# A hybrid decoder layer: the last stage goes tile by tile, and the square-root table is loaded by a dummy operation

## The chip, the cores and the metric

The kernel runs on one core of one Trainium2 chip. The metric is the device time of one execution in microseconds, given as the median of several runs. One core has a matrix engine (TensorE, "PE" in the profile, its weight loads "PEld"), VectorE ("DVE"), ScalarE ("ACT"), GpSimd ("POOL") and SyncE ("SP"), which here issues nearly all transfers. The engines run on their own and meet at semaphores. TensorE writes its products into PSUM, eight banks of 128 partitions by 512 float32 words.

## The reference, cut to what matters

The layer takes 256 prompt tokens and 8 times 8 sample tokens, 320 rows of 1024 features. After a DeltaNet branch, a chunk-MLP branch and a mixture of experts, the stage that the change touches computes this:

```python
def rmsnorm(x, g):
    y = x * rsqrt(mean(x * x, axis=-1, keepdims=True) + EPS)
    return y * g

x = x + moe_ffn(h2, ...)                       # 32 experts, top 4
h3 = rmsnorm(x, norm3_g)
x = x + sigmoid(h3 @ ple_gate_w) * (p[i] @ ple_w)   # gate 1024x1024, ple 256x1024
y = rmsnorm(x, final_norm_g)                   # written out for prompt and samples
```

## The kernel before, in words

All work is float32. The 320 tokens form three tiles (`TILES`): 0 and 1 are the prompt's two halves of 128 tokens, 2 is the 64 samples. The kernel is written by hand as one instruction stream for each engine; inside a stream the order of the code is the order of execution, and a stream stops only at its own `wait_ge` on a semaphore.

The first 600 us hold both branches and the router. Then a loop (L1005 on TensorE, L1320 on ScalarE, L1765 on VectorE) goes over 35 blocks of 64 chosen tokens, with weights that SyncE streams in. The combined result of the experts stays in PSUM banks 0 to 4 (0 and 1: tile 0; 2 and 3: tile 1; 4: the samples).

What follows the loop is the tail, L1056 to L1106 on TensorE:

- `combine(nb + 1)` (L1056) adds the last block, and six transposes (L1060) turn the per-layer embedding `p` into banks 5 and 6. ScalarE copies them to `pT` (L1334).
- VectorE copies the summed `x` out of PSUM, tile 0, tile 1, samples (L1784 to L1786). ScalarE makes for each tile the sum of squares and the root (`rms`, L1120 and L1121). VectorE takes the reciprocal and scales (`normalise`, L1373 and L1374), which gives `h2`, the rows of h3 without their gain.
- The tail has ten products, numbered n = 0 to 4 twice. Tile 0 has n = 0 and 1 (the halves of the 1024 output columns), tile 1 has 2 and 3, the samples have 4, where both halves lie above each other in one bank. The first five are `p @ ple_w` (two steps of k each); the other five are the gate logits `h3 @ ple_gate_w` (eight steps each).
- `turn_h3` (L1079) transposes h2 for all three tiles, one k after the other, 24 transposes (L1087) through three banks. ScalarE evacuates even k (L1340), VectorE odd k (L1793), both with the gain `g3`. All 24 must be done before the first gate product (L1099, L1100).
- Each finished gate product goes through a sigmoid on ScalarE (L1345), a multiplication with the ple product (L1800) and an addition to `x` (L1803; for the samples L1807 to L1809, since the second half has to be moved down by 64 partitions). After the last product of a tile the final norm follows: squares and root (L1120, L1121), reciprocal and scaling (L1812, L1813), and a store by SyncE (L505). Sigmoid and root lie in different activation tables, so ScalarE has a table load at each change.

The order is fixed: gate products 0, 1, 2, 3, 4, so tile 0, tile 1, samples last.

Of the kernel before, what the change touches and what calls it, by code (L numbers as in the profile page):

```python
# [90 lines left out]
def hybrid_layer(nc, t):  # L91
    ctx = ExitStack()
    with ctx:
# [200 lines left out]
        PLE_BANKS = (5, 6, 7, 0, 1)  # L294
        H3_BANKS = (2, 3, 4)
        GATE_BANKS = (2, 3)
# [101 lines left out]
        def _(sp):  # L398
# [103 lines left out]
            for tt, (t0, tn) in enumerate(TILES):  # L502
                sp.wait_ge(sem("y_ready"), tt + 1)
                dst = t["out_yp"][0, t0:t0 + tn, :] if tt < 2 else t["out_ys"].rearrange("b s d -> (b s) d")
                sp.dma_start(dst, x[0:tn, tt, :]).then_inc(sem("stored"), 16)  # L505
# [123 lines left out]
        def _(pe):  # L629
# [436 lines left out]
            def ple_products(n, bank, lhsT, weights, kn):  # L1066

# [3 lines left out]
                for k in range(kn):  # L1071
                    if tt < 2:
                        m = mm(ps[:, bank, :], lhsT[:, k, t0:t0 + tn], weights(k, n % 2), k == 0, k == kn - 1)
                    else:
                        for g in range(2):
                            m = mm(ps[64 * g:64 * g + 64, bank, :], lhsT[:, k, t0:t0 + tn], weights(k, g), k == 0, k == kn - 1)
                return m

            def turn_h3(ks):  # L1079

                pe.wait_ge(sem("xn_ready"), 9)
                for k in ks:
                    if k >= 3:
                        odd = (k - 3) % 2
                        pe.wait_ge(sem(("hT_ready", "hT_odd_ready")[odd]), KD + odd + (k - 3) // 2 + 1)
                    for tt, (t0, tn) in enumerate(TILES):
                        m = pe.transpose(ps[:, H3_BANKS[k % 3], t0:t0 + tn], h2[0:tn, tt, k * P:(k + 1) * P], ident[0:tn, 0:tn])  # L1087
                    m.then_inc(sem("hT_done"), 1)
# [12 lines left out]
            for half in range(2):  # L1101
                pe.wait_ge(landed[uslot[half]], 16 * (before[uslot[half]] + NE + 1))
            for n in range(5):
                if n >= 2:
                    pe.wait_ge(sem("ple_sig_ready"), n - 1)
                ple_products(n, GATE_BANKS[n % 2], h3T, lambda k, g: slots[uslot[g]][:, k, :], KD).then_inc(sem("ple_done"), 1)  # L1106

# [4 lines left out]
        def _(act):  # L1112
# [222 lines left out]
            for tt in range(3):  # L1335
                act.wait_ge(sem("x_summed"), tt + 1)
# [4 lines left out]
            for n in range(5):  # L1341
                act.wait_ge(sem("ple_done"), 5 + n + 1)
                if n >= 2:
                    act.wait_ge(sem("ple_added"), n - 1)
                ACTF([g_sb, u_sb][n % 2], ps[:, GATE_BANKS[n % 2], :], ACT.Sigmoid).then_inc(sem("ple_sig_ready"), 1)  # L1345
                if n % 2 or n == 4:

                    tt = n // 2
# [493 lines left out]
```

## Time and profile before

| | us |
|---|---|
| median of 3 runs | 1681.19 |
| lowest, highest | 1679.02, 1683.44 |
| the profiled execution, its own time | 1679.4 |
| its span in the trace | 1677.6 |
| TensorE busy in the span | 1612.6 (96%) |
| TensorE's mean granted clock | 0.987 of full |

The profiled execution took 1.8 us more than its span. The tail, from the last `combine` to the end of the span, is 1611.1 to 1677.6 us. The page names for each engine its busy time, cuts the span into 40 slices, and follows the chain of work that ended last; the timeline, the stretches with their granted clock, and the chain of a window come from the trace.

### The profile page before, as it was taken

To read this page: it belongs to the slowest core of one execution; us is meant where nothing else is said; L and a number is where in the kernel's file an instruction comes from. 1 tells how busy PE (TensorE), PEld (TensorE's weight loads), DVE (VectorE), ACT (ScalarE), POOL (GpSimd) and SP (SyncE) were. 2 spreads that over 40 slices of the span, in tenths; PEclk is the share of its full clock that TensorE was granted. 3 is DMA by queue.
4 is the path that set the end of the run, shared out by engine and by line. 5 is a ranking of instruction groups with operands and counts; after the bars stand their busy time and mean duration, and the time that the engine had idled before them with its cause. 6 is when DMAs were issued, how large, how long until landed. Compare 5 with 4: busy or idle time off the path is not lost.

```text
span 1677.6 us, 21022 instructions
## 1 busy us (share of the span) xinstructions
PE 1612.6 (96%) x8487; PEld 751.6 (45%) x8488; DVE 458.6 (27%) x966; ACT 316.9 (19%) x529; POOL 112.1 (7%) x150
## 2 busy tenths in 40 slices
PE   7999999999979999999999999999999999999997
PEld 4677776776555433333333333333333333333332
DVE  3665322224771421111111112111121111112122
ACT  2224131123400131111111111111011111111123
POOL 1322101012150030000000000000000000000000
PEclk9999999999989999999999999999999999999999
DMA  4334212125854579996999999999999979949940
GB/s 160 111 121 128 102 51 102 51 101 163 255 150 168 240 285 420 417 378 258 419 419 416 419 417 418 419 416 419 417 418 419 416 311 364 419 194 408 415 146 31
DMA packets 112366, 477.32 MB, mean 285 GB/s; under 512 B 7386, under 2 KB 18067, under 8 KB 79475
## 3 DMA queue, kind: packets, MB, share of 16 engines
q1 hardware_dynamic: 109846, 467.64, 70.4%
q0 software_dynamic: 2480, 9.11, 1.9%
q8 instruction: 29, 0.48, 0.1%
q14 instruction: 11, 0.09, 0.0%
HBM read 469.72 MB, written 6.62 MB: 284 GB/s over the span
## 4 chain that ended last, share of the span: by engine, by line
PE 72%; DMA 21%; DVE 4%; issue 1%; ACT 1%; SPq 0%; ACTq 0%; DVEq 0%
PE ps L631 69%; DMA arena<-in_moe_w 20%; PE ps L981 1%; ACT arena L1307 1%; PE ps L1053 1%; DVE arena L1525 1%; PE ps L649 0%; DMA arena<-in_state_conv 0%; DVE arena L1620 0%; DVE arena L1559 0%; DVE arena L1522 0%; PE ps L1087 0%; PE ps L703 0%; DVE arena L1563 0%; DVE arena L1589 0%
## 5 line engine op out<-in xcount | busy, mean ns | idle before, releaser
L631 PE MATMUL ps<-arena 128*64 128x512 f32 (+12 forms) x7898 | 1521.4, 476 | 37.8 <-DMA arena<-in_moe_w 17.0
L631 PEld LDWEIGHTS ps<-arena 128*64 128x64 f32 (+6 forms) x7898 | 687.0, 148 | 842.0 <-issue 663.3
L1774 DVE TENSOR_SCALAR arena<-ps 128x512 f32<-128x512 f32 x35 | 24.2, 692 | 446.2 <-PE ps L631 446.2
L1322 ACT ACTIVATE arena<-arena 128x512 f32<-128x512 f32 x35 | 22.0, 630 | 475.4 <-DVE arena L1774 475.4
L1767 DVE COPY arena<-arena 96x64 bf16 x35 | 6.7, 191 | 251.6 <-PE ps L1053 248.1
L1327 ACT ACTIVATE arena<-ps 128x512 f32<-128x512 f32 x35 | 20.9, 597 | 261.6 <-PE ps L631 261.6
L1758 DVE TENSOR_TENSOR arena<-ps,arena 128x512 f32<-128x512 f32 x36 | 24.9, 692 | 122.7 <-PE ps L981 121.6
L1307 ACT ACTIVATE arena<-ps 128x512 f32<-128x512 f32 x36 | 21.5, 597 | 134.4 <-PE ps L631 134.4
L1322 ACT ACT_TABLE_LOAD x35 | 44.9, 1283 | 0.6
L1409 DVE SCALAR_TENSOR_TENSOR arena<-arena 128x344 f32<-128x344 f32 x48 | 35.5, 740 | 1.7
L1120 ACT ACTIVATE arena<-arena 128x1024 f32<-128x1024 f32 (+1 forms) x12 | 12.6, 1052 | 113.8 <-DVE arena L1644 103.3
L1190 ACT ACTIVATE arena<-ps 128x320 f32<-128x320 f32 x32 | 14.0, 436 | 98.0 <-PE ps L631 97.8
L1769 DVE TENSOR_SCALAR arena<-arena 128x128 f32<-128x128 f32 (+1 forms) x105 | 29.8, 342 | 0.0
L981 PE MATMUL ps<-arena 128*128 128x128 f32 x144 | 23.6, 287 | 3.7
L1780 DVE TENSOR_TENSOR arena<-arena 128x512 f32<-128x512 f32 x35 | 24.3, 694 | 1.2
L1777 DVE SCALAR_TENSOR_TENSOR arena<-arena 128x512 f32<-128x512 f32 x35 | 24.3, 693 | 1.2
L1053 PEld LDWEIGHTS ps<-arena 128*128 128x128 f32 (+1 forms) x105 | 11.8, 140 | 27.8 <-issue 27.8
L1775 DVE TENSOR_SCALAR arena<-ps 128x512 f32<-128x512 f32 x35 | 23.8, 681 | 0.0
L1503 DVE TENSOR_TENSOR arena<-arena,ps 128x512 f32<-128x512 f32 (+1 forms) x11 | 7.6, 687 | 59.2 <-PE ps L631 59.2
L1031 PE MATMUL ps<-arena 128*128 128x128 f32 x140 | 23.0, 287 | 0.0
L581 POOL TENSOR_TENSOR arena<-arena 128x512 f32<-128x512 f32 (+1 forms) x15 | 18.9, 1266 | 55.7 <-PE ps L631 27.0
L1053 PE MATMUL ps<-arena 128*128 128x128 f32 (+1 forms) x105 | 22.5, 292 | 0.0
(249 smaller groups left out, 649.3 us busy)
## 6 DMA issues: line engine op xcount, KB each, us to landing
arena<-in_moe_w SPq DMA_DIRECT2D x192, 2048.0 KB, 18.3
arena<-in_w_in SPq DMA_DIRECT2D x16, 2048.0 KB, 11.1
arena<-in_state_delta POOLq DMA_DIRECT2D x16, 512.0 KB, 6.3
arena<-in_w_proj_a SPq DMA_DIRECT2D x2, 2048.0 KB, 11.1
out_sd_s<-arena SPq DMA_DIRECT2D x8, 512.0 KB, 5.8
arena<-in_w_proj_b SPq DMA_DIRECT2D x2, 2048.0 KB, 11.5
arena<-in_w_out SPq DMA_DIRECT2D x2, 2048.0 KB, 7.8
arena<-in_ple_gate_w SPq DMA_DIRECT2D x2, 2048.0 KB, 16.0
```

Of the source, the lines that this page charges most:

```text
L631: return pe.matmul(out, lhsT, rhs, start=first, stop=last, skip_group_check=True)
L981: m = pe.transpose(ps[:, TURN_B, P * j:P * j + P], xsel[:, P * j:P * j + P], ident)
L1053: m = pe.transpose(ps[:, TURN_B, t0:t0 + tn], Pg[0:tn, tt, :], ident[0:tn, 0:tn])
L1307: ACTF(xsel, ps[:, TURN_B, :], ACT.Copy).then_inc(sem("xsel_ready"), 1)
L1322: ACTF(s_sb, g_sb, ACT.Sigmoid, scale=ALPHA).then_inc(sem("glu_sig_ready"), 1)
L1409: ch.link(STT(a, z[:, i:i + CW], g_conv[:, i, n:n + 1], a, ALU.mult, ALU.add))
L1758: TT(xselT.rearrange("p (g j) s -> p g j s", g=2), ps[:, TURN_B, :].rearrange("p (j g s) -> p g j s", j=4, g=2), g2.rearrange("p (g j a) - ...
L1769: m = TS(Pg[0:tn, tt, :], cst("slot", tn), posb[0:tn, tt, bass.ds(b, 1)], gateb[0:tn, tt, bass.ds(b, 1)], ALU.is_equal, ALU.mult)
L1774: TS(g_sb, ps[:, GATE_B, :], LIMIT, None, ALU.min).then_inc(sem("glu_gate_ready"), 1)
L1775: TS(u_sb, ps[:, UP_B, :], LIMIT, -LIMIT, ALU.min, ALU.max).then_inc(sem("glu_up_ready"), 1)
L1777: STT(u_sb, u_sb, 1.0, g_sb, ALU.add, ALU.mult).then_inc(sem("glu_up_ready"), 1)
L1780: TT(a_sb, u_sb, s_sb, ALU.mult).then_inc(sem("act_ready"), 1)
```

## The change

Only the tail is touched.

- The tiles go in the order 2, 0, 1 (samples first) in the copies out of PSUM, in the norm, in the transposes, in the gate products (n = 4, 0, 1, 2, 3) and in the stores.
- h3 is transposed tile by tile, eight transposes each, into whole banks: samples into bank 4, tile 0 into 2 and 3, tile 1 into 4 and 7. VectorE alone evacuates them, with one instruction for a bank. ScalarE's four evacuations are gone.
- TensorE's stream is: ple 4, turn samples, ple 0, first half of gate 4, turn tile 0, second half of gate 4, ple 1, gate 0, turn tile 1, ple 2, ple 3, gate 1, gate 2, gate 3.
- Each product has its own bank or a bank that a finished product left, so the gate products wait on `ple_added` instead of on the sigmoids.
- ScalarE runs a root of one column (`ACTF(warm, eps_col, ACT.Sqrt)`) right after the loop and after each sigmoid that ends a tile; nothing reads its result.

```diff
+        TAIL_TILES = (2, 0, 1)
+        TAIL_ORDER = (4, 0, 1, 2, 3)
+        PLE_BANKS = {4: 7, 0: 5, 1: 6, 2: 0, 3: 1}
+        LOGIT_BANKS = {4: 4, 0: 2, 1: 3, 2: 5, 3: 6}
+        H3_BANKS = {2: (4,), 0: (2, 3), 1: (4, 7)}
...
-            for n in range(5):
-                if n == 0:
-                    pe.wait_ge(sem("pT_ready"), 2)
-                elif n == 3:
-                    pe.wait_ge(sem("x_summed"), 1)
-                elif n == 4:
-                    turn_h3(range(3))
-                ple_products(n, PLE_BANKS[n], pT, lambda k, g: wp[:, k, 512 * g:512 * g + 512], 2).then_inc(sem("ple_done"), 1)
-            turn_h3(range(3, KD))
-            pe.wait_ge(sem("hT_ready"), KD + KD // 2)
-            pe.wait_ge(sem("hT_odd_ready"), KD + 1 + KD // 2)
...
+            def turn_h3(tt):
+                tn = TILES[tt][1]
+                banks = H3_BANKS[tt]
+                per = KD // len(banks)
+                for k in range(KD):
+                    m = pe.transpose(ps[:, banks[k // per], tn * (k % per):tn * (k % per) + tn], h2[0:tn, tt, k * P:(k + 1) * P], ident[0:tn, 0:tn])
+                    if k % per == per - 1:
+                        m.then_inc(sem("hT_done"), 1)
+
+            pe.wait_ge(sem("pT_ready"), 2)
+            ple_product(4)
+            pe.wait_ge(sem("xn_ready"), 7)
+            turn_h3(2)
+            ple_product(0)
...
+            pe.wait_ge(sem("hT_odd_ready"), KD + 2)
+            gate_logits(4, range(KD // 2))
+            pe.wait_ge(sem("x_summed"), 3)
+            pe.wait_ge(sem("xn_ready"), 8)
+            turn_h3(0)
+            gate_logits(4, range(KD // 2, KD))
+            ple_product(1)
+            pe.wait_ge(sem("hT_odd_ready"), KD + 4)
+            gate_logits(0)
+            pe.wait_ge(sem("ple_added"), 1)
+            pe.wait_ge(sem("xn_ready"), 9)
+            turn_h3(1)
+            ple_product(2)
+            ple_product(3)
+            gate_logits(1)
+            pe.wait_ge(sem("hT_odd_ready"), KD + 6)
+            pe.wait_ge(sem("ple_added"), 2)
+            gate_logits(2)
+            pe.wait_ge(sem("ple_added"), 3)
+            gate_logits(3)
...
+            ACTF(warm, eps_col, ACT.Sqrt)
             act.wait_ge(sem("pT_done"), 1)
...
-            for k in range(0, KD, 2):
-                act.wait_ge(sem("hT_done"), 2 * KD + 1 + k + 1)
-                ACTF(h3T[:, k, :], ps[:, H3_BANKS[k % 3], 0:TOK], ACT.Copy, scale=g3[:, k:k + 1]).then_inc(sem("hT_ready"), 1)
...
+            for i, n in enumerate(TAIL_ORDER):
+                act.wait_ge(sem("logits_done"), 2 + i + 1)
+                if i >= 2:
+                    act.wait_ge(sem("ple_added"), i - 1)
+                ACTF([g_sb, u_sb][i % 2], ps[:, LOGIT_BANKS[n], :], ACT.Sigmoid).then_inc(sem("ple_sig_ready"), 1)
                 if n % 2 or n == 4:
+                    ACTF(warm, eps_col, ACT.Sqrt)
+                    act.wait_ge(sem("ple_added"), i + 1)
+                    rms(n // 2, h2[:, n // 2, :])
...
+            ch(dve.tensor_copy(x[0:64, 2, 0:512], ps[0:64, 4, :]))
+            dve.tensor_copy(x[0:64, 2, 512:1024], ps[64:128, 4, :]).then_inc(sem("x_summed"), 1)
             for tt in range(2):
                 dve.tensor_copy(x[:, tt, :], ps[:, 2 * tt:2 * tt + 2, :].rearrange("p a c -> p (a c)")).then_inc(sem("x_summed"), 1)
-            ch(dve.tensor_copy(x[0:64, 2, 0:512], ps[0:64, 4, :]))
-            dve.tensor_copy(x[0:64, 2, 512:1024], ps[64:128, 4, :]).then_inc(sem("x_summed"), 1)
             ch.wait()
+            dve.wait_ge(sem("x_summed"), 3)
+            def h3_turned(tt, done):
+                t0, tn = TILES[tt]
+                banks = H3_BANKS[tt]
+                per = KD // len(banks)
+                for a, bank in enumerate(banks):
+                    dve.wait_ge(sem("hT_done"), 2 * KD + 1 + done + a + 1)
+                    TT(h3T[:, per * a:per * a + per, t0:t0 + tn], ps[:, bank, :].rearrange("p (k s) -> p k s", k=per),
+                       g3[:, per * a:per * a + per].rearrange("p (k a) -> p k a", a=1).broadcast_to([P, per, tn]), ALU.mult).then_inc(sem("hT_odd_ready"), 1)
+            normalise(3, 2, h2, TAIL_TILES)
+            h3_turned(2, 0)
+            normalise(3, 0, h2, TAIL_TILES)
+            h3_turned(0, 1)
+            normalise(3, 1, h2, TAIL_TILES)
...
+                if i == 0:
+                    h3_turned(1, 3)
```

How the order moves, first on TensorE at the head of the tail. L631 is the helper that issues every product, L1060 turns `p`, L1087 turns h3. A product of the prompt's tiles has 128 rows, one of the samples is written as 64x512 twice. Before:

```order
L1060 MATMUL ps<-arena 128x64
L631 MATMUL ps<-arena 128x512 x8
L1087 MATMUL ps<-arena 128x128 x2
L1087 MATMUL ps<-arena 128x64
...
L631 MATMUL ps<-arena 64x512 x4
...
L631 MATMUL ps<-arena 128x512 x32
L631 MATMUL ps<-arena 64x512 x16
```

In the changed kernel the same engine has (L634 and L1063 are the old L631 and L1060, L1095 is the new transposes):

```order
L1063 MATMUL ps<-arena 128x64
L634 MATMUL ps<-arena 64x512 x4
L1095 MATMUL ps<-arena 128x64 x8
L634 MATMUL ps<-arena 128x512 x2
L634 MATMUL ps<-arena 64x512 x8
L1095 MATMUL ps<-arena 128x128 x8
L634 MATMUL ps<-arena 64x512 x8
L634 MATMUL ps<-arena 128x512 x10
L1095 MATMUL ps<-arena 128x128 x8
L634 MATMUL ps<-arena 128x512 x28
```

The ple product of the samples alone now stands ahead of the first transposes, and the 24 transposes are three groups of eight with products between them.

ScalarE after the last gate product, before (L1345 is the sigmoid, L1120 the squares, L1121 the root):

```order
L1345 ACTIVATE arena<-ps 128x512 [waits ple_done]
L1120 ACTIVATE arena<-arena 64x1024 [waits ple_added]
L1121 ACT_TABLE_LOAD
L1121 ACTIVATE arena<-arena 64x1 [waits act_chain]
L93 UNCONDITIONAL_BRANCH
```

and in the changed kernel (L1362, L1139 and L1140 are those three, L1365 is the dummy root):

```order
L1362 ACTIVATE arena<-ps 128x512 [waits ple_added,logits_done]
L1365 ACT_TABLE_LOAD
L1365 ACTIVATE arena<-arena 128x1
L1139 ACTIVATE arena<-arena 128x1024 [waits ple_added]
L1140 ACTIVATE arena<-arena 128x1 [waits act_chain]
L93 UNCONDITIONAL_BRANCH
```

The table load has moved ahead of the wait for `ple_added` and of the squares.

## Rows read from the trace of the kernel before

**Rows 1.** The page, costliest groups: count, busy us, mean ns, idle before.
```profile
L1758 DVE TENSOR_TENSOR arena<-ps,arena 128x512 f32<-128x512 f32 x36 | 24.9, 692 | 122.7 <-PE ps L981 121.6
```

**Rows 2.** Chain that ended last, head of the tail: start us, us, what.
```profile
1616.17 7.11 PE ps L631 x16
1623.28 1.57 PE ps L1087 x9
1624.85 1.87 PE ps L631 x8
1626.71 2.87 PE ps L1087 x15
1629.58 0.69 issue
1630.27 36.41 PE ps L631 x96
```

**Rows 3.** Stretches: PE, PEld, DVE, ACT, POOL busy, granted clock, DMA share, GB/s.
```profile
1614.00:1616.00 2.00, 1.23 (x8) 0.67 (x6) 1.87 (x2) 0.74 (x3) 0.00 (x0) 1.00 0.00 0
...
1628.00:1630.00 2.00, 1.58 (x9) 0.81 (x7) 0.94 (x2) 1.36 (x3) 0.00 (x0) 1.00 0.00 0
1630.00:1632.00 2.00, 1.73 (x2) 0.84 (x3) 0.17 (x1) 0.87 (x1) 0.00 (x0) 0.55 0.00 0
```

**Rows 4.** Timeline of ScalarE, 1638 to 1647 us: sigmoids of gate products 0 and 1.
```profile
1639.07 0.60 ACT L1345 ACTIVATE arena<-ps 128x512 f32<-128x512 f32 x1 [8.20 <-PE ps L631]
1645.94 0.60 ACT L1345 ACTIVATE arena<-ps 128x512 f32<-128x512 f32 x1 [6.27 <-PE ps L631]
```

**Rows 5.** Timeline, 1614 to 1620 us, VectorE and ScalarE: start, us, what.
```profile
1614.13 2.36 DVE L1784 COPY arena<-ps 128x1024 f32<-128x1024 f32 x2 [10.81 <-PE ps L631]
...
1615.91 1.06 ACT L1120 ACTIVATE arena<-arena 128x1024 f32<-128x1024 f32 x1
...
1616.40 0.67 DVE L1785 COPY arena<-ps 64x512 f32<-64x512 f32 x1
...
1617.08 1.28 ACT L1121 ACT_TABLE_LOAD   x1
...
1618.38 0.29 ACT L1121 ACTIVATE arena<-arena 128x1 f32<-128x1 f32 x1
...
1618.77 0.16 DVE L1373 RECIPROCAL arena<-arena 128x1 f32<-128x1 f32 x1 [0.97 <-ACT arena L1121]
...
1618.97 0.75 DVE L1374 TENSOR_SCALAR arena<-arena 128x1024 f32<-128x1024 f32 x1
```

**Rows 6.** TensorE's timeline near 141 us, and half-microsecond stretches as in Rows 3.
```profile
141.05 4.45 PE L703 MATMUL ps<-arena 128*27 128x128 f32 x24
...
144.50:145.00 0.50, 0.50 (x4) 0.40 (x3) 0.00 (x0) 0.50 (x1) 0.00 (x0) 0.50 0.60 233
145.00:145.50 0.50, 0.50 (x4) 0.45 (x3) 0.00 (x0) 0.49 (x3) 0.00 (x0) 0.60 0.74 254
```

**Rows 7.** Chain that ended last, end of the tail: start us, us, what.
```profile
1666.70 0.61 ACT arena L1345
...
1668.05 0.42 DVE arena L1807
...
1668.51 0.69 DVE arena L1808
...
1669.94 1.15 ACT arena L1120 x2
...
1671.11 1.28 ACT L1121
```

**Rows 8.** Issues of the stores: KB each, median us from issue to landing; and the last store.
```profile
out_yp<-arena SPq DMA_DIRECT2D x2, 512.0 KB, 2.6
...
out_ys<-arena SPq DMA_DIRECT2D x1, 256.0 KB, 2.9
...
1674.22 0.51 SPq L505 DMA_DIRECT2D out_ys<-arena  x1
```

More of the change, by code:

```diff
@@ L500, in _ @@
             sp.dma_start(fng, t["final_norm_g"].rearrange("(a d) -> a d", a=1).broadcast_to([P, D])).then_inc(sem("ple_in"), 16)
-            for tt, (t0, tn) in enumerate(TILES):
-                sp.wait_ge(sem("y_ready"), tt + 1)
+            for i, tt in enumerate(TAIL_TILES):
+                t0, tn = TILES[tt]
+                sp.wait_ge(sem("y_ready"), i + 1)
                 dst = t["out_yp"][0, t0:t0 + tn, :] if tt < 2 else t["out_ys"].rearrange("b s d -> (b s) d")
@@ L1064, in _, with products @@
             wp = slots[uslot[2]].rearrange("p k n -> p (k n)")[:, 0:2048].rearrange("p (k n) -> p k n", k=2)
-            def ple_products(n, bank, lhsT, weights, kn):
+            def products(n, bank, lhsT, weights, ks, last):
                 tt = min(n // 2, 2)
                 t0, tn = TILES[tt]
-                for k in range(kn):
+                for k in ks:
                     if tt < 2:
-                        m = mm(ps[:, bank, :], lhsT[:, k, t0:t0 + tn], weights(k, n % 2), k == 0, k == kn - 1)
+                        m = mm(ps[:, bank, :], lhsT[:, k, t0:t0 + tn], weights(k, n % 2), k == 0, k == last)
@@ L1074, in ple_products @@
                     else:
                         for g in range(2):
-                            m = mm(ps[64 * g:64 * g + 64, bank, :], lhsT[:, k, t0:t0 + tn], weights(k, g), k == 0, k == kn - 1)
+                            m = mm(ps[64 * g:64 * g + 64, bank, :], lhsT[:, k, t0:t0 + tn], weights(k, g), k == 0, k == last)
                 return m
[L1079 to L1088, printed above, removed]
@@ L1090, in _, with ple_product @@
-            for n in range(5):
-                if n == 0:
-                    pe.wait_ge(sem("pT_ready"), 2)
-                elif n == 3:
-                    pe.wait_ge(sem("x_summed"), 1)
-                elif n == 4:
-                    turn_h3(range(3))
-                ple_products(n, PLE_BANKS[n], pT, lambda k, g: wp[:, k, 512 * g:512 * g + 512], 2).then_inc(sem("ple_done"), 1)
-            turn_h3(range(3, KD))
-            pe.wait_ge(sem("hT_ready"), KD + KD // 2)
-            pe.wait_ge(sem("hT_odd_ready"), KD + 1 + KD // 2)
+            def ple_product(n):
+                products(n, PLE_BANKS[n], pT, lambda k, g: wp[:, k, 512 * g:512 * g + 512], range(2), 1).then_inc(sem("ple_done"), 1)
@@ new lines, in gate_logits @@
+            def gate_logits(n, ks=range(KD)):
+                m = products(n, LOGIT_BANKS[n], h3T, lambda k, g: slots[uslot[g]][:, k, :], ks, KD - 1)
+                if ks[-1] == KD - 1:
+                    m.then_inc(sem("logits_done"), 1)
+            def turn_h3(tt):
[6 more added lines that the diff above has]
+                        m.then_inc(sem("hT_done"), 1)
@@ L1368, in _, with normalise @@
             dve.memset(ab, 0.0).then_inc(sem("zeroed"), 1)
-            def normalise(k, tt, dst):
+            def normalise(k, tt, dst, order=(0, 1, 2)):
                 tn = TILES[tt][1]
-                dve.wait_ge(sem("rms_ready"), 3 * (k - 1) + tt + 1)
+                dve.wait_ge(sem("rms_ready"), 3 * (k - 1) + order.index(tt) + 1)
                 ch.link(dve.reciprocal(rstd[0:tn, tt:tt + 1], rstd[0:tn, tt:tt + 1]))
```

35 lines of the change are left out of this document (8 added, 27 removed).

## The prediction, made before the changed kernel ran

> **What bounds the kernel now.** I read the chain of work that ended last first. At its end it lies in the tail: TensorE from 1616.17 us to the last gate product at 1630.27 + 36.41 = 1666.68 [rows 2], with one hole of 0.69 us before the gate products, then eleven microseconds that alternate between ScalarE and VectorE [rows 7] and end in the store of the samples, issued at 1674.22 [rows 8], with the span's end at 1677.6. So two things count: what makes TensorE reach its last product earlier, and what lies behind that product. Whatever ScalarE and VectorE do beside the gate products costs nothing. Everything ahead of 1614 us is the same in both kernels, so of 1680 us only some 65 are open.
>
> The second view is the stretches with their granted clock. The gate products begin at half clock (1.2 of 2.4 GHz): 0.55 as the mean of 1630 to 1632 us, after 1.00 up to 1630 [rows 3]. What TensorE did before it fell was fifteen transposes and the hole [rows 2]. The price comes from the sigmoids. Gate product 1 took 1645.94 - 1639.07 = 6.87 us; product 0 took 1639.07 - 1630.27 = 8.80 [rows 4]. The last product, with its drain, takes 36.41 - 8.80 - 3 x 6.87 = 7.00, so the slow stretch cost 8.80 - 7.00 = 1.80 us.
>
> **The head of the tail on TensorE.** The ten products are the same, and so is the number of transposes, 24, which took 1.57 + 2.87 = 4.44 us [rows 2]. Four things differ.
>
> The hole before the gate products goes: -0.69. Product, turned bank and evacuation are now apart. The samples' bank is evacuated during ple 0, tile 0's two banks during gate 4's second half, tile 1's during ple 2, ple 3 and gate 1. One such evacuation is a 128x512 operation of VectorE out of PSUM with a broadcast factor, 0.69 us [rows 1], against two steps of ple 0, which take 7.11 / 4 = 1.8 us. Without that cover it would cost 0.7 for each group. Next in line is `ple_added`: the samples' additions are over about 4 us after gate 4, and TensorE asks for them after 1.8 + 6.9 us of products. VectorE then waits for the turning of tile 1 with the samples' final norm queued behind it; that norm is needed only by a store, with four gate products still to come.
>
> A new wait comes in. After ple 4, TensorE wants the samples' h2. It is free at 1616.17 + 1.87 = 1618.04. VectorE has first its three copies, 2 x 0.67 for the samples and 2.36 for tiles 0 and 1, from 1614.13: until 1617.9 with gaps. ScalarE's squares can start at 1615.91 as now and take 1.15 with the read of the sum [rows 5, 7], and the root, its table now loaded before, 0.29: ready at 1617.4. So VectorE is later. Reciprocal 0.16 and scaling 0.75 [rows 5] end at 1618.9. TensorE waits 0.9 us; queued behind it are all the gate products. If the root came with its load (1.28) [rows 5], this would be 1.7, and if the copies cost nothing, 0.4. I take 0.9, since every duration in it has a row.
>
> Cutting the work into more pieces costs some filling at each change between transposes and products. Of the four ple products in a row each took 7.11 / 4 = 1.78; ple 4, between transposes, took 1.87 [rows 2]: 0.1 at such a place. Two more such places than before make 0.2. From below: the samples' eight transposes have a quarter of the data, and if they ran in half the time of the others (4.44 x 8 / 24 / 2) it would be 0.7 less. I take +0.2, by the row that it is nearest to.
>
> The slow stretch. Before, fifteen transposes stood together just ahead of the hole. Now no group is longer than eight transposes (about 1.5 us), and each has products on both sides. The quietest place is new: the transposes of `p`, the wait for `pT` until 1616.17 [rows 2], ple 4, 0.9 of waiting, eight small transposes, then ple 0. The first half of that exists already, and the clock stayed at 1.00 from 1614 to 1616 with TensorE busy for 1.23 of 2 us [rows 3]. So I let the slow stretch go: -1.80. The bounds are -1.80 and 0 (it comes at the new quiet place).
>
> The Trainium skill has a rule here ("TensorE: Matmul & The Clock Gate", Part 4, PE-mode transpose): transposes do not count as busy for the clock in the way products do. By that rule the chip would see only ple 4 between 1614 and 1620 us, and the slow stretch would move there, not go: the sum would be 1.80 worse.
>
> The trace bears out both sides. The clock fell here after transposes and a hole [rows 2, 3]. But at 145 us it came back, from 0.50 to 0.60 and then 1.00, while TensorE had done nothing but the transposes of L703 for four microseconds [rows 6]. So transposes alone can bring the clock back, and I don't take the fall for certain.
>
> Head: -0.69 + 0.9 + 0.2 - 1.80 = -1.4, so the last product ends at 1665.3.
>
> **Behind the last product.** With the samples last there were, after the sigmoid, a multiplication, the move by 64 partitions (0.42 + 0.03 gap), two additions (0.69 each) and after the squares the table load of 1.28 [rows 7]. With tile 1 last, the move and one addition go: -0.45 - 0.71. The load goes from this place: -1.28. It is now issued behind the sigmoid, with the dummy root: 1.28 + 0.29 + 0.02 = 1.59, beside a multiplication and an addition on VectorE (0.69 + 0.70 + gaps = 1.43). The cover is short by 0.16: +0.16. The last store is 512 KB in place of 256 KB, but the large ones landed in 2.6 us and the small one in 2.9 [rows 8]: -0.3; the bounds are -0.3 and +0.3, should twice the bytes count after all. Squares and scaling are as long for 64 partitions as for 128 (1.06 us for a 128-row tile against 1.15 with the read of the sum for 64) [rows 5, 7]. Sum: -2.6.
>
> The skill ("ScalarE: Activation LUTs", What ACT_TABLE_LOAD costs) gives a switch of tables 1283 ns and a drain of about 1380 ns more. With that the dummy would stick out by 1.5 us, and this part would bring 1.2. The trace has the 1.28 but no drain: the root follows the load at 1617.08 + 1.28 + 0.02 = 1618.38 [rows 5].
>
> **The sum.** -1.4 - 2.6 = -4.0 us. Against the profiled execution's own 1679.4 that is 1675.4. That execution lies 1.8 below the median of the three runs, and nothing says that the next ones will be as low, so I put the sum against the median: 1681.19 - 4.0 = 1677.2.
>
> **The rivals.**
>
> The slow stretch stays, at the new quiet place or wherever it falls: no gain from it, -2.2 us, 1679.0. For it: between 1614 us and ple 0, nearly six microseconds, only ple 4's 1.9 are products. Against it: the stretch before 1616 us kept its clock, and the fall at 1630 us had a longer row of transposes without a product between. It would give the same time if the executions of before mostly don't have the stretch.
>
> Every group of transposes now costs one: three slow stretches in place of none, -4.0 + 3 x 1.80 = +1.4, 1682.6, slower than before. It decides with the third stretch: one leaves 2.2 of the gain, two leave 0.4, three turn it over. For it: the clock fell behind transposes. Against it: the groups at tile 0 and 1 have at least 3.4 us of products on each side.
>
> The change brings the lower bounds: small transposes in half the time, no filling, the dummy covered: -4.0 - 0.7 - 0.2 - 0.16 = -5.1, 1676.1. For it: only the smaller amount of data; against it: every group of transposes in the chain took 0.17 to 0.19 us each, small ones included.
>
> The dummy roots don't do their work (the head's root still carries its load, or the one at the end sits in the way): 0.8 more in the head and 1.3 at the end, -1.9, 1679.3. The order of the compiled code speaks against it: load and dummy stand ahead of the waits.
>
> **How the numbers follow.** Forecast, stretch gone: 0.50. Stretch stays: 0.28. Lower bounds: 0.12. Dummies without effect: 0.04. Three stretches: 0.06. Likeliest is 1677.2. The range reaches over the second case and the third and adds the median's own scatter (three runs of before lie 4.4 us apart, so a median of three moves by 1 or 2): 1674.5 to 1681.5. A measurement of this kernel can tell about 0.3% from no change, which is 5.0 us, so faster means under 1676.1. That takes half of the lower-bound case (0.06), a fifth of the forecast's (0.10) and a little of the others': 0.18. Slower by over 0.3% (over 1686.2) needs more than three stretches: 0.02. The rest, 0.80, is within 0.3%.
>
> **What would show it.** Right: TensorE stands still for about 0.9 us ahead of the samples' transposes, released by VectorE's scaling; no wait before any gate product; a granted clock of 1.00 from 1616 us to the last product, which ends some 50 us after `combine`, 1.4 sooner than before; behind it 10.9 - 2.6 = 8.3 us to the end of the span, with a load beside VectorE's multiplication. Wrong: a granted clock near 0.5 around 1620 us, a wait before a gate product, a store that takes 3 us or more, or an end behind the last product of more than 9.5 us.

## The result, and the profile after

The changed kernel took 1674.60 us (median of 6 runs, 1673.28 to 1675.03), the kernel before 1681.38 us beside it; the ratio is 0.9959, with a 95% interval of 0.9948 to 0.9971. That is 6.8 us less, where 4.0 were forecast. The measured time lies at the low edge of the range (1674.5 to 1681.5), and it is faster by more than 0.3%, a case that had a chance of 0.18.

Two later comparisons on other occasions gave 0.9981 (0.9970 to 0.9992) and 0.9963 (0.9950 to 0.9977). Over all three, 21 runs of the changed kernel have a median of 1674.6, and 66 runs of before, taken beside all experiments, 1680.0: 5.4 us.

One execution of either program scatters by several microseconds, and the traces show where: the first block of the loop turns its activations (L1031) at 612.8 us in the trace of before, at 616.3 in a second trace of the same program, at 618.2 in another kernel with the same front. The loop behind it then takes about as long in each of them (997.6 to 999.3 us to the last combine, in the ten traces with this loop and this combine). So I compare tails, from the start of the last combine to the end of the span. Before that is 1677.6 - 1611.09 = 66.5 us.

The page of the changed kernel, its first line and the costliest group:

```profile
span 1672.8 us, 21024 instructions
...
PE 1612.1 (96%) x8487; PEld 752.2 (45%) x8488; DVE 456.4 (27%) x967; ACT 315.5 (19%) x529; POOL 112.1 (7%) x150
```

The chain that ended last, changed kernel, from the last combine on (start us, us, what; the answer to [rows 2] and [rows 7]):

```profile
1612.20 3.02 PE ps L634 x12
...
1619.32 0.76 DVE arena L1391
...
1620.12 0.71 PE ps L1095 x8
1620.83 5.50 PE ps L634 x20
1626.33 1.02 PE ps L1095 x8
1627.35 12.37 PE ps L634 x36
1639.72 0.87 PE ps L1095 x8
1640.59 24.05 PE ps L634 x56
...
1664.66 0.60 ACT arena L1362
...
1665.28 1.28 ACT L1365
...
1666.57 0.20 ACT arena L1365
1666.78 1.12 ACT arena L1139 x2
...
1667.92 0.30 ACT arena L1140
...
1668.45 1.29 DVE arena L1843
```

The tail is 1672.8 - 1612.20 = 60.6 us, 5.9 less. L634 are the products and L1095 the transposes of h3. From 1620.12 on TensorE has no gap up to the last product, at 1664.64; before the first group of transposes stands VectorE's scaling (L1391), for which TensorE waited 0.90 us, in the row of TensorE's own timeline:

```profile
1620.12 0.71 PE L1095 MATMUL ps<-arena 64*128 64x64 f32 x8 [0.90 <-DVE arena L1391]
```

The granted clock of the changed kernel, at the new quiet place and where the old slow stretch was (columns as in [rows 3]):

```profile
1618.00:1620.00 2.00, 1.22 (x6) 0.17 (x2) 1.88 (x3) 1.94 (x7) 0.00 (x0) 1.00 0.00 0
1620.00:1622.00 2.00, 1.88 (x11) 1.25 (x12) 1.16 (x4) 1.95 (x4) 0.00 (x0) 1.00 0.00 0
...
1630.00:1632.00 2.00, 2.00 (x9) 0.71 (x6) 0.39 (x1) 1.00 (x2) 0.00 (x0) 1.00 0.00 0
```

It stays at full speed, where [rows 3] has 0.55.

From the start of the combine to the end of the last product there are 52.4 us in place of 55.6, so -3.15 (forecast -1.4). The terms are the holes, -0.69 + 0.90; the transposes, 0.71 + 1.02 + 0.87 = 2.60 us in place of 4.44, so -1.84; and the products, 43.9 us (the three groups of the chain and 1.94 for ple 4) in place of 45.4 [rows 2], so -1.54, the slow stretch and some filling together. Behind the last product there are 8.16 us in place of 10.92, so -2.76 (forecast -2.6).

### The profile page after: what moved, and what is told of

It reads as the page before. It is cut to its first block, busy times and chain, and to the rows that moved or that the text cites. A ratio compares the mean times of both kernels' runs of the same rounds, so it can differ in the third digit from the quotient of the medians.

```text
span 1672.8 us, 21024 instructions
## 1 busy us (share of the span) xinstructions
PE 1612.1 (96%) x8487; PEld 752.2 (45%) x8488; DVE 456.4 (27%) x967; ACT 315.5 (19%) x529; POOL 112.1 (7%) x150
## 4 chain that ended last, share of the span: by engine, by line
PE 71%; DMA 21%; DVE 4%; issue 1%; ACT 1%; POOL 1%; SPq 0%; POOLq 0%; DVEq 0%; ACTq 0%
PE ps L634 68%; DMA arena<-in_moe_w 20%; PE ps L984 1%; ACT arena L1326 1%; PE ps L1056 1%; POOL arena L626 1%; DVE arena L1542 1%; PE ps L652 0%; DMA arena<-in_state_conv 0%; DVE arena L1576 0%; DVE arena L1637 0%; DVE arena L1539 0%; PE ps L706 0%; DVE arena L1580 0%; DVE arena L1606 0%
## 5 line engine op out<-in xcount | busy, mean ns | idle before, releaser
L634 PE MATMUL ps<-arena 128*64 128x512 f32 (+12 forms) x7898 | 1522.5, 476 | 35.4 <-DMA arena<-in_moe_w 16.1
L634 PEld LDWEIGHTS ps<-arena 128*64 128x64 f32 (+6 forms) x7898 | 687.8, 148 | 839.3 <-issue 663.1
L1139 ACT ACTIVATE arena<-arena 128x1024 f32<-128x1024 f32 (+1 forms) x12 | 12.6, 1051 | 107.7 <-DVE arena L1661 101.7
## 6 DMA issues: line engine op xcount, KB each, us to landing
arena<-in_w_proj_b SPq DMA_DIRECT2D x2, 2048.0 KB, 11.5
```

Source lines behind the costliest of these rows:

```text
L634: return pe.matmul(out, lhsT, rhs, start=first, stop=last, skip_group_check=True)
```

## The experiments

Twelve runs were made, on three occasions: nine edited kernels, the changed kernel twice and the kernel before once. The table has the wall times and the tails of the traces, each from one execution; "clock" says whether TensorE's granted clock fell to half inside the tail, ahead of the last product. No tail is given where the edit moves the combine, from whose start it is counted.

| kernel | median us (runs) | ratio to before beside it, 95% | tail us | clock |
|---|---|---|---|---|
| before_again | 1683.17 (1) | | 66.4 | fell |
| e_dummies_only | 1679.57 (10) | 0.9992, 0.9982 to 1.0002 | 65.1 | fell |
| e_no_dummies | 1678.37 (10) | 0.9991, 0.9981 to 1.0000 | 62.7 | full |
| e_together | 1676.97 (8) | 0.9977, 0.9966 to 0.9988 | 61.2 | full |
| after_again | 1676.44 (10) | 0.9981, 0.9970 to 0.9992 | 60.6 | full |
| e_grouped_rows | 1681.43 (10) | 1.0002, 0.9991 to 1.0014 | 64.0 | full |
| e_patterns | 1679.19 (1) | | 60.6 | full |
| e_filled_head | 1675.76 (10) | 0.9972, 0.9960 to 0.9983 | | fell |
| after_third | 1673.79 (5) | 0.9963, 0.9950 to 0.9977 | 60.6 | full |
| e_loop_rows | 1673.63 (6) | 0.9967, 0.9955 to 0.9979 | 60.6 | full |
| e_best | 1672.78 (6) | 0.9958, 0.9944 to 0.9973 | | full |
| e_best_loop | 1670.08 (5) | 0.9945, 0.9931 to 0.9959 | | full |

**before_again**: the kernel before, not edited.

> The kernel before, unchanged, for a second trace. The result of the change was 1674.6 us against 1681.4 (-6.8) where -4.0 was forecast, while the two profiled tails (from the last combine to the end of the span) differ by 66.5 - 60.6 = 5.9. If the slow stretch of the clock after the transposes belongs to this order of work, the second trace has it again, between 15 and 24 us after the combine, and the tail is again 66 to 67 us. If it comes by chance, the tail is either 66.5 without a change of time elsewhere or about 64.7 with a granted clock of 1.00 throughout. If more than one stretch can fall into the tail (which would explain why the executions of before scatter over 4.4 us and those of after over 1.8), it is up to 68.3.

The tail is 66.4 us again, and the slow stretch again follows the transposes. The scatter is not in the tail but ahead of it: this trace is 1.7 us later than the first by 567 us and 3.5 later by 616. What differs on the way are slow stretches of the clock between 574 and 600 us, where the router's small operations leave TensorE waiting; they lie at other places in the two traces (around 582 and 590 us in the first, around 576, 586 and 594 in the second).

**e_dummies_only**: before, plus the dummy roots.

```diff
+            ACTF(warm, eps_col, ACT.Sqrt)
             act.wait_ge(sem("pT_done"), 1)
...
                     tt = n // 2
+                    ACTF(warm, eps_col, ACT.Sqrt)
                     act.wait_ge(sem("ple_added"), n + 1)
```

> The kernel before plus only the dummy roots (behind the loop and behind the last sigmoid of each tile). Theory: at the head nothing changes, since TensorE has ple products to do until h2 is there; at the end the load of 1.28 us leaves the chain, covered by the four VectorE operations of the samples (2.6 us): -1.3 us, about 1680.1, and the root follows the squares within 0.05 us. Rival one (a switch of tables costs a drain besides its load, which the trace doesn't show): -2.7. Rival two (a dummy delays the squares by itself): -1.0 or less.

The tail is 65.1 us, 1.3 to 1.4 less, as expected from the load's own 1.28. The median is 0.5 us less (1680.07 to 1679.57), inside its noise. Rival one, the drain, asked for 2.7 and is out by the tails; the medians alone could not tell. The chain has squares and root with nothing between:

```profile
1672.01 1.16 ACT arena L1120 x2
1673.17 0.02 issue
1673.19 0.30 ACT arena L1121
```

The slow stretch is in this trace too. So it is in three of three traces of this order of work.

**e_no_dummies**: the changed kernel without them (the two `ACTF(warm, ...)` lines of the diff above taken out of it).

> The changed kernel without its dummy roots. Theory: at the end the load is back in the chain, +1.28, and the dummy's own delay of about 0.06 goes: +1.2; at the head the first root comes at 1619.8 in place of 1618.5 in the trace's time, while VectorE is free at 1619.1, so TensorE waits 1.6 in place of 0.9: +0.7. Sum +1.9, about 1676.5. Rival (the head is not bound by the root): +1.2, about 1675.8, and the wait stays at 0.9.

The tail is 62.7, so +2.1 against 60.6 (expected +1.9). Both parts are in the chain: ScalarE's load now stands ahead of the samples' root and holds VectorE back, and it stands again behind the last squares.

```profile
1618.86 1.02 ACT arena L1139 x2
...
1619.90 1.28 ACT L1140
...
1621.20 0.30 ACT arena L1140
```

So the dummies are worth 2.1 us in the changed order, and 1.3 in the old one, where nothing at the head waits for the root. The median lies 1.7 below before where the tails differ by 3.7; a difference of 2 between the two ways of looking is more than I can account for. The 2.1 us rest on the traces.

**e_together**: ple products first, then all transposes tile by tile, then the gate products.

```diff
-        LOGIT_BANKS = {4: 4, 0: 2, 1: 3, 2: 5, 3: 6}
-        H3_BANKS = {2: (4,), 0: (2, 3), 1: (4, 7)}
+        LOGIT_BANKS = {4: 3, 0: 2, 1: 4, 2: 5, 3: 6}
+        H3_BANKS = {2: (4,), 0: (2, 3), 1: (4, 2)}
...
+            for n in (4, 0, 1, 2, 3):
+                if n == 2:
+                    pe.wait_ge(sem("x_summed"), 3)
+                ple_product(n)
+            pe.wait_ge(sem("xn_ready"), 9)
+            turn_h3(2)
+            turn_h3(0)
+            pe.wait_ge(sem("hT_odd_ready"), KD + 3)
+            turn_h3(1)
...
+            pe.wait_ge(sem("hT_odd_ready"), KD + 6)
+            gate_logits(4)
...
```

> The changed kernel with its five ple products first, then all 24 transposes (still tile by tile), then the five gate products; three banks are used twice. Theory, that products between the groups keep the clock up: the slow stretch is back, +1.8; a hole of 1.4 us before the gate products and up to 0.5 at the third group, while the new wait of 0.9 is gone: +1.0. Sum +2.8, about 1677.4, with a granted clock near 0.5 behind the transposes. Rival, that the shorter time of the transposes alone (2.6 us for 24, against 4.4 before) keeps the clock: +1.0, about 1675.6, and a clock of 1.00. The transposes take 2.6 us under both; if they take 4.4, it was the products between them that made them fast.

My theory fell here. From the last ple product at 1631.38 to the first gate product at 1635.54 there are 4.16 us of transposes and holes, longer than the 3.56 of before, and the clock stayed full (columns as in [rows 3]):

```profile
1630.00:1632.00 2.00, 2.00 (x13) 0.94 (x11) 0.00 (x0) 0.00 (x0) 0.00 (x0) 1.00 0.00 0
1632.00:1634.00 2.00, 1.64 (x14) 1.41 (x14) 1.89 (x3) 0.00 (x0) 0.00 (x0) 1.00 0.00 0
1634.00:1636.00 2.00, 0.96 (x8) 0.50 (x8) 1.29 (x2) 0.00 (x0) 0.00 (x0) 1.00 0.00 0
```

The tail is 61.2, +0.6 against the changed kernel; the rival had said +1.0. So "products between the transposes" brings 0.6 us, the evacuations that it covers, and is not needed for the full clock in this trace. The medians agree with the tails: 1676.97, and 1676.44 for the changed kernel in after_again.

**after_again** and **after_third**: the changed kernel, not edited.

> The changed kernel once more, beside the same runs of the kernel before as the three others. The tails of the traces differ by 5.9 us (66.5 to 60.6); the first comparison gave 6.8. If the 0.9 above the tails is scatter of the first 600 us (the first block of the loop turned its rows at 612.8 to 618.0 us in six traces of kernels whose front is the same), this run is 5.9 within about 1 below before, and its tail is 60.6 within 0.2. If the change moves something ahead of the tail, it is again 6.8 or more.

The tail is 60.6 again, as expected. The difference of the medians is 3.4 us where 5.9 within 1 was expected, with an interval of 1.3 to 5.0, which doesn't hold the 5.9 of the tails; in this set the changed kernel scattered from 1674.25 to 1680.11.

> The changed kernel beside the three others, as their base on this chip. So far its tail is 60.6 us in two traces against 66.5 and 66.4 of before, and the differences of the medians were 6.8 and 3.4 us. The front of the same program ends anywhere from 612.8 to 618.4 us in ten traces, with slow stretches of the clock in other places each time, so a median of ten runs moves by about 1. Expected: 5.9 below before, within 1.5.

The median is 5.5 us below before, and the tail 60.6. Two of the three comparisons have the 5.9 in their interval, and all runs together give 5.4.

**e_grouped_rows**: before, with the transposes of each round taken tile by tile.

```diff
...
-                    for tt, (t0, tn) in enumerate(TILES):
-                        m = pe.transpose(ps[:, H3_BANKS[k % 3], t0:t0 + tn], h2[0:tn, tt, k * P:(k + 1) * P], ident[0:tn, 0:tn])
-                    m.then_inc(sem("hT_done"), 1)
+                for tt, (t0, tn) in enumerate(TILES):
+                    for k in part:
+                        m = pe.transpose(ps[:, H3_BANKS[k % 3], t0:t0 + tn], h2[0:tn, tt, k * P:(k + 1) * P], ident[0:tn, 0:tn])
+                        if tt == 2:
+                            m.then_inc(sem("hT_done"), 1)
```

> The kernel before, with its transposes in the same three rounds of k, the same banks and the same evacuations, but inside a round tile by tile in place of k by k. So weights of 128 rows are followed by weights of 64 rows 3 times in place of 8, nothing else changes. Theory (the 1.8 us that the transposes of h3 got shorter come from these changes of rows: the trace of before has a pause of 0.17 us ahead of the weight load of each 64-row transpose and none in between): -5 x 0.17 = -0.85, the 24 transposes take 3.6 us in place of 4.44. Rival (it is the change of bank, which each transpose still makes): 4.4 as before. On the clock: if the fall needs the whole length of the transposes, it may stay away, and then it is -1.8 more.

The first nine transposes, which wait for no evacuation, take 0.98 us in place of 1.57 [rows 2], with the same banks and the same data:

```profile
1629.26 0.98 PE ps L1091 x9
1630.24 1.87 PE ps L631 x8
1632.11 1.09 PE ps L1091 x8
...
1633.89 0.84 PE ps L1091 x5
...
1635.48 34.75 PE ps L631 x96
```

All 24 take 2.9 us in place of 4.4, less than the 3.6 expected: a visit to 64 rows costs more than its pause of 0.17. Now they catch up with the evacuations, and some of it goes into holes. The rival, the change of bank, is out. The last 96 products are the same as before and take 34.75 us at full clock in place of 36.41 [rows 2], so the slow stretch cost 1.66 us. The tail is 64.0, 2.4 less. The median did not follow (1681.43 against 1679.87 of before). This trace has a late front (618.2 us), but why ten runs show nothing of the shorter tail stays open; whether the slow stretch was in those without a trace can't be seen. So the full clock of this order stands on one trace.

**e_patterns**: the changed kernel with 48 transposes more behind the last product; nothing reads their results.

```diff
             gate_logits(3)
+            for i in range(12):
+                pe.transpose(ps[:, 2, 0:P], h3T[:, i % 8, 0:P], ident)
+            for i in range(12):
+                pe.transpose(ps[:, 2 + i % 3, 0:P], h3T[:, i % 8, 0:P], ident)
+            for i in range(12):
+                pe.transpose(ps[:, 2, 0:64], h3T[0:64, i % 8, 0:P], ident[0:64, 0:64])
+            for i in range(6):
+                pe.transpose(ps[:, 2, 0:P], h3T[:, i % 8, 0:P], ident)
+                pe.transpose(ps[:, 2, 128:192], h3T[0:64, i % 8, 0:P], ident[0:64, 0:64])
```

> The changed kernel with 48 more transposes on TensorE behind the last gate product, beside the final norm: 12 of 128x128 into one bank, 12 of 128x128 into three banks in turn, 12 of 64 rows into one bank, 12 that alternate 128 and 64 rows in one bank. They are beside the path, so the time is that of the changed kernel (within 0.5). Theory (weights of 64 rows behind 128 rows wait for the products in flight): 1.4 us for the first group (0.11 each), the same for the second, 0.9 for the third (0.07 each), 2.1 for the fourth, with 0.17 ahead of each of its six 64-row transposes. Rival (change of bank): the second group takes 2.5 and the fourth 1.1.

The single run took 1679.19 us, 2.8 above the median of after_again where 0.5 was allowed; its front was late (618.4 us) and its tail is 60.6 as in the changed kernel. The chain ends in the added transposes, so it lists each group (L1127 one bank, L1129 three banks, L1131 64 rows, L1133 and L1134 alternating):

```profile
1669.18 1.31 PE ps L1127 x12
1670.49 1.31 PE ps L1129 x12
1671.80 0.89 PE ps L1131 x12
1672.69 0.26 PE ps L1133
1672.96 0.20 PE ps L1134
1673.16 0.26 PE ps L1133
```

This is the direct measurement. A transpose of 128 rows takes 0.109 us whether it changes its bank or not, one of 64 rows 0.074. Alternating, a pair takes 0.46 where 0.18 would be the sum: a visit to 64 rows between 128 rows costs 0.28, split over both changes. Before had eight such visits in the transposes of h3, each with a second 128-row transpose: three transposes then take 0.109 + 0.26 + 0.20 = 0.57, and eight times that is 4.56, near the 4.44 of [rows 2].

The same trace says something of the clock. From 1669.18 to 1675.47 us, for more than six microseconds, TensorE did transposes alone, and the clock stayed full; it fell once they were over.

```profile
1672.00:1674.00 2.00, 2.00 (x18) 1.38 (x15) 1.16 (x2) 0.74 (x3) 0.00 (x0) 1.00 0.00 0
1674.00:1676.00 2.00, 1.48 (x7) 0.82 (x6) 0.29 (x1) 0.00 (x0) 0.00 (x0) 1.00 0.43 178
1676.00:1678.00 2.00, 0.00 (x0) 0.00 (x0) 0.00 (x0) 0.00 (x0) 0.00 (x0) 0.75 0.21 84
```

**e_filled_head**: the transposes of p ahead of the combine, three ple products ahead of the first transposes of h3.

```diff
-        P_BANKS = (5, 6)
+        P_BANKS = (5, 7)
...
-            combine(nb + 1)
             pe.wait_ge(sem("ple_in"), 48)
             for k in range(2):
+                if k == 1:
+                    pe.wait_ge(sem("ysb_ready"), nb + 1)
...
+            combine(nb + 1)
...
             ple_product(4)
+            ple_product(0)
+            ple_product(1)
+            pe.wait_ge(sem("x_summed"), 3)
             pe.wait_ge(sem("xn_ready"), 7)
             turn_h3(2)
-            ple_product(0)
+            ple_product(2)
...
-            ple_product(1)
+            ple_product(3)
...
-            ple_product(2)
-            ple_product(3)
```

> A version meant to beat both. The transposes of p stand ahead of the last combine (their second half into bank 7), where TensorE waits for ScalarE anyway, so that pT is copied during the combine; then ple 4, 0, 1 stand ahead of the samples' transposes, ple 2 behind them, ple 3 behind gate 4. Theory: the hole of 0.95 us for pT goes, that of 0.90 for h2 shrinks (h2 is there 4.9 us after the combine, TensorE has 5.4 us of products), and of the 1.2 us of the transposes of p some 0.6 lie in the hole of 0.62: tail 60.6 - 0.95 - 0.90 - 0.6 = 58.2. Rival: the dummy's table load (1.28) now stands ahead of the copies of pT only by 1 us and all of it is still hidden; if not, pT comes late and 0.5 stays. A second: with fewer holes nothing else is left to fill, but h2 of the samples is late by the copies, +0.3.

A transfer took the place of the holes. `ple_in` counts three transfers, and the broadcast of the final gain, issued last, landed after 11 us; combine and everything behind it now stood behind that wait. Behind it the clock was at half:

```profile
1615.27 0.99 PE L1064 MATMUL ps<-arena 128*128 128x128 f32 x3 [2.27 <-DMA arena<-in_final_norm_g]
```

```profile
1616.00:1618.00 2.00, 2.00 (x8) 1.13 (x10) 0.00 (x0) 0.77 (x2) 0.00 (x0) 0.50 0.00 0
1618.00:1620.00 2.00, 2.00 (x8) 0.70 (x4) 0.00 (x0) 0.00 (x0) 0.00 (x0) 0.50 0.00 0
```

From the loop's last transposes of Pg (1612.36 us) to the end of the span this trace has 64.7 us, the changed kernel's 61.9, where 2.4 less was expected. Neither of my rivals was this one. The traced execution was the slowest of the ten, and their median lies 0.7 below that of after_again, so this wait need not have been in all of them.

**e_loop_rows**: the changed kernel, transposes of Pg with 128 rows in the loop.

```diff
+            dve.memset(Pg[64:128, 2, :], 0.0)
...
-                    m = pe.transpose(ps[:, TURN_B, t0:t0 + tn], Pg[0:tn, tt, :], ident[0:tn, 0:tn])
+                    m = pe.transpose(ps[:, TURN_B, t0:t0 + P], Pg[:, tt, :], ident)
```

> The changed kernel, and in each of the 35 blocks of the loop the three transposes of Pg all with 128 rows (the samples' tile has zeros below its 64 rows), where the third had 64. The extra transposes behind the last product showed what a change between 128 and 64 rows costs: 0.26 and 0.20 us for an alternating pair where two of a kind take 0.11 and 0.07, so 0.28 for one visit to 64 rows. Theory: 35 x (0.28 - 0.04) = -8.4 us if TensorE alone bounds the loop. Rival: the weights' transfers run at 416 to 419 GB/s in most slices, and a faster TensorE only waits longer for them: -1 or 0. I expect something between, about -3. The three transposes and what follows start 0.2 us sooner in each block in any case.

From the loop's first transposes of activations (612.1 and 612.5 us) to the last combine the two traces take 997.8 and 996.4 us: 1.3 less. Unchanged loops scatter by 1.7 us (997.6 to 999.3), so this is little more than scatter, and the medians, 1673.79 and 1673.63, don't tell the two apart. The rival comes nearest, but a part of the answer was in neither: a block gains less than the 0.24 us of the theory. In the block at 1110 us the three transposes and what follows take 1110.56 - 1109.99 = 0.57 us in after_third and 1110.41 - 1109.93 = 0.48 in this kernel, 0.09 less:

```profile
1109.99 0.64 PE L1056 MATMUL ps<-arena 128*128 128x128 f32 x3
1110.56 10.66 PE L634 MATMUL ps<-arena 128*64 128x512 f32 x48
```

```profile
1109.93 0.55 PE L1056 MATMUL ps<-arena 128*128 128x128 f32 x3
1110.41 10.76 PE L634 MATMUL ps<-arena 128*64 128x512 f32 x48
```

What follows the 64-row transpose here is a product and not a 128-row transpose, so the price of a visit taken from e_patterns doesn't carry over. And 13 times in the loop TensorE waits for the experts' weights (up to 1.3 us, in both traces), where even the 0.09 is lost: a block with such a wait takes 30.1 us in both kernels, one without it 28.44 and 28.35.

**e_best**: e_filled_head, with the wait for p alone, and the final gain multiplied in ahead of the root for tile 1.

```diff
-            sp.dma_start(fng, t["final_norm_g"].rearrange("(a d) -> a d", a=1).broadcast_to([P, D])).then_inc(sem("ple_in"), 16)
+            sp.dma_start(fng, t["final_norm_g"].rearrange("(a d) -> a d", a=1).broadcast_to([P, D])).then_inc(sem("fng_in"), 16)
...
-                sp.dma_start(dst, x[0:tn, tt, :]).then_inc(sem("stored"), 16)
+                sp.dma_start(dst, h2[:, 0, :] if tt == 1 else x[0:tn, tt, :]).then_inc(sem("stored"), 16)
...
-            pe.wait_ge(sem("ple_in"), 48)
+            pe.wait_ge(sem("ple_in"), 32)
...
+                    if n == 3:
+                        dve.wait_ge(sem("ple_added"), 5)
+                        ch.link(TT(h2[:, 0, :], x[:, 1, :], fng, ALU.mult))
...
+                        TS(h2[:, 0, :], h2[:, 0, :], rstd[:, 1:2], None, ALU.mult).then_inc(sem("y_ready"), 1)
```

> The version with the filled head once more, mended: the transposes of p wait for p alone and not for the broadcast of the final gain, which landed 11 us after its issue and held TensorE for 2.3 us (with the clock at half for six after it). Besides, x times the final gain of tile 1 is made while ScalarE sums the squares, so that behind the root there is one scaling (0.75 us) in place of the operation of 1.29. Theory: from the end of the loop's last transposes (1611.6 in the changed kernel's first trace) to the end 61.2 - 0.95 - 0.9 - 0.6 - 0.5 = 58.2 us, so -3.0 against the changed kernel. Rival: p itself lands late (10 to 11 us after an issue at 1598 to 1599), with 1 us or more of waiting ahead of the combine, and half of the gain goes.

Measured from the loop's last transposes of Pg to the end of the span, the changed kernel has 1672.8 - 1610.94 = 61.9 us and e_best 1670.7 - 1611.84 = 58.9: -3.0, as expected. The median is only 1.0 less than after_third's, and the six runs (1670.05 to 1675.77) reach past its five on both sides, so the wall times don't show the gain. The clock stays full. The transfer of p lands 11.5 us after its issue, at 1612.48, and releases the first transposes at 1612.53: it comes just in time here, and could hold TensorE up in another execution. From there TensorE is without a gap of more than 0.1 us to the last product, and the last scaling takes 0.75:

```profile
1600.97 11.51 DMA arena<-in_p_sample
...
1612.53 1.21 PE ps L1064 x6
1613.74 8.28 PE ps L634 x28
1622.02 0.64 PE ps L1097 x8
...
1666.91 0.75 DVE arena L1851
```

**e_best_loop**: e_best and e_loop_rows together.

> e_best and e_loop_rows together: the sum of the two differences within 1 us, since one is in the loop and the other behind it. Rival: a loop that ends sooner leaves p less time to land, and the gain of e_best shrinks by what the loop gained in its last block (0.2).

The median is 1670.08 us, 3.7 below after_third and 9.3 below before beside it (ratio 0.9945). By the medians the two differences were 1.0 and 0.2, so the expected sum within 1 us was missed; by the traces they were 3.0 and 1.3, which fits. It is the fastest kernel of the study; its range, 1669.14 to 1672.32, lies at or below every run of after_third. By its trace the part from the last transposes of Pg on is 1668.9 - 1610.33 = 58.6 us.

## Why the prediction was right or wrong

The sign and most of the mechanism held; the size was too small, and with it the chance of more than 0.3%. The step that failed is one term of the sum, the time of the 24 transposes.

- The hole before the gate products went, as predicted, and so did the wait before any gate product. -0.69.
- The new wait was worked out as 0.9 and measured as 0.90, released by VectorE's scaling. e_no_dummies shows that the root would have been next, with 0.8 more.
- **The transposes are the step that failed.** I kept their 4.44 us, wrote that the number of transposes is the same, and gave 0.7 as the lower bound. They took 2.60. A transpose's price depends on what stands before it: the old order alternated 128 and 64 rows, the new one doesn't. e_patterns and e_grouped_rows show this apart from the rest of the change. My argument for 4.44, that every group in the chain took 0.17 to 0.19 us for each transpose, small ones included, came from groups in which both kinds alternate. It was to be read in the trace of before, where weight loads of the transposes have a pause of 0.17 us ahead of each 64-row one and none between others (the second line is three loads in a row, one of 64 rows and the two of 128 that follow):

```profile
1623.12 0.14 PEld L1087 LDWEIGHTS ps<-arena 128*128 128x128 f32 x1 [0.29 <-issue]
1623.42 0.40 PEld L1087 LDWEIGHTS ps<-arena 64*128 64x128 f32 x3 [0.17 <-issue]
```

- The same trace has both kinds by themselves, in the router: sixteen 128-row transposes in a row (L931), whose starts go from 565.0 to 566.7 us, 0.11 apart, and eight 64-row ones (L939) in 0.71 us, exactly what the samples' group then took:

```profile
565.00 1.97 PE L931 MATMUL ps<-arena 128*128 128x128 f32 x16
...
570.47 0.71 PE L939 MATMUL ps<-arena 64*128 64x64 f32 x8
```

  I took the price of the group that the change removes and not of the one that it makes. With these rows the 24 come to 16 x 0.11 + 0.71 = 2.5 in place of 4.44, and the sum to -4.0 - 2.0 = -6.0, against the 5.9 of the tails.
- The slow stretch and the filling were put at -1.80 + 0.2 = -1.6 and came to -1.54 together. With the 1.66 of e_grouped_rows for the stretch, 0.12 is left for the filling: both were a little too large, and part of the good fit is that these errors cancel.
- The slow stretch went, but my reason for it fell. It followed the transposes in three of three traces of the old order, and is in no trace of the kernels with shorter transposes except e_filled_head, which waited 2.3 us for a transfer. e_together had all transposes in a row with holes, 4.16 us, and kept its clock; e_patterns had six of nothing but transposes and kept it. What e_together, e_grouped_rows and the changed kernel share is that transposes follow each other closely. That this is the cause is argued, not shown: none of these kernels was made with slow transposes and products between, and e_together and e_grouped_rows have one trace each, so chance is not excluded for them.
- In e_patterns the granted clock was 1.00 through six microseconds of nothing but transposes. By the rule of the Trainium skill that transposes don't count as busy for the clock ("TensorE: Matmul & The Clock Gate", Part 4, PE-mode transpose) it would have fallen during them; the trace does not agree.
- Behind the last product -2.6 was forecast and -2.76 measured. The move, the addition and the load went as worked out. The dummy cost 0.05 and not 0.16: its operation took 0.20 us (I had put it at 0.29) and the squares followed at 1666.78, while VectorE's addition ended at 1666.71, with 0.02 to add for a start behind it. From the end of the scaling, 1669.74, to the end of the span the store took 3.06 us, before 3.4, for twice the bytes. My sign of being wrong, a store of 3 us or more, did not say from where to count: from issue to landing the page has 2.6 for the stores of 512 KB, as before.
- Taking a load off the path brought 1.3 us in e_dummies_only, not 2.7. The drain that the Trainium skill adds to a load ("ScalarE: Activation LUTs", What ACT_TABLE_LOAD costs) is in no trace here.
- The last 0.9 of the first comparison, 6.8 against 5.9, lies inside its interval (4.9 to 8.7): the second comparison gave 3.4 and the third 5.5. That it comes from the scatter ahead of the tail is likely, not shown. The mended sum gives 6.0, not 6.8.

Of the rivals, "three slow stretches", "the dummies without effect" and "the stretch stays" did not happen. "The lower bounds" (-5.1) was nearest, but its bound for the transposes was 1.1 us short.

## What to carry to other kernels

Price an operation by the neighbours that it will have, not by those that it had: look for a group of the same kind in the new arrangement elsewhere in the trace. Transposes of one shape are cheaper when they stand together, and a tail that ends in alternating engines gets shorter by taking table loads, gains and moves out of the part behind the last product. When something is pulled ahead of a wait, ask which transfers its semaphore counts. A price measured between two neighbours holds for these neighbours: the gain of 0.24 us that I carried from e_patterns into the loop was 0.09 there.

## What the runs showed of the hardware

Between float32 transposes of 128 rows, which take 0.109 us each in a row, one of 64 rows (0.074 in a row) costs TensorE about 0.28 us more for the visit and back (e_patterns). A change of PSUM bank costs nothing there: twelve take 1.31 us either way. Where a product follows the 64-row transpose, making it one of 128 rows gained 0.09 us (e_loop_rows). Transposes close together, and nothing else, went with a granted clock of 1.00 for over six microseconds (e_patterns). A table load of 1.28 us that a dummy root takes off the path is worth 1.3 us at the end of the tail, and no more (e_dummies_only). The loop began between 612.1 and 618.4 us in the fourteen traces, with practically the same code ahead of it, so differences in the tail are read better from traces than from a few medians.
